# Pooling on VectorE between attention units, seeds written by ScalarE, readout's parts in the recurrence's last chunk

## What is computed

```python
def pool_mixer(u, pool_w, pool_scale):
    cs = jnp.concatenate([jnp.zeros_like(uf[:, :1]), jnp.cumsum(uf, axis=1)], axis=1)
    for gi, w in enumerate(POOL_WINDOWS):
        mean = (jnp.take(csg, hi, axis=1) - jnp.take(csg, lo, axis=1)) / (hi - lo)[None, :, None]
        outs.append((mean - uf[..., sl]).astype(u.dtype) @ pool_w[gi])
    return jnp.concatenate(outs, axis=-1) * pool_scale
```

```python
def step(S, inp):
    S = (S * w_t[:, :, None, :]
         - jnp.einsum('bhij,bhj->bhi', S, kk_t)[..., None] * kka_t[:, :, None, :]
         + v_t[..., None] * k_t[:, :, None, :])
def rwkv_readout(y, r, k_sum, v, g, r_k, ln_g, ln_b, wo, dtype):
    mean = jnp.mean(y, axis=-1, keepdims=True)
    var = jnp.mean(jnp.square(y - mean), axis=-1, keepdims=True)
    yn = ((y - mean) * lax.rsqrt(var + GN_EPS)).reshape(B, L, D_MODEL) * ln_g + ln_b
    bonus = (jnp.sum(r * k_sum * r_k, axis=-1, keepdims=True) * v).reshape(B, L, D_MODEL)
    return ((yn + bonus) * g).astype(dtype) @ wo
```

## Time and profile before

| what | us |
|---|---|
| median of 3 runs | 2590.53 (2588.93 to 2593.68) |
| the profiled run | 2590.95 |
| span of its profile | 2589.1 |
| PE busy in the span | 2378.9 (92%) |
| DVE busy | 1719.1 (66%) |
| ACT busy | 1011.7 (39%) |
| POOL busy | 68.1 (3%) |

### The profile page before, as it was taken

One profiled execution on the slowest core, in us unless ns is written; L12 is line 12 of the kernel. 1 busy time (PEld: TensorE's weight loads), 2 busy tenths in 40 slices (PEclk: granted clock), 3 DMA queues, 4 the chain that ended last, 5 costly groups with the idle time before them and its releaser, 6 DMA issues.

```text
span 2589.1 us, 46659 instructions
## 1 busy us (share of the span) xinstructions
PE 2378.9 (92%) x20102; PEld 1954.2 (75%) x20102; DVE 1719.1 (66%) x3313; ACT 1011.7 (39%) x1879; POOL 68.1 (3%) x70
## 2 busy tenths in 40 slices
PE   6899978999988999999999889898889989998998
PEld 5775457787866578888887789895677889677886
DVE  6966789667646247787773677765365865755576
ACT  2125242313322223543331453344345654644465
POOL 0300000000000000000000000020000011000000
PEclk9899989999998999999998999999989999997999
DMA  7430426555541100000002477640045943003574
GB/s 306 146 114 1 174 103 240 221 221 211 211 154 67 64 1 3 3 4 3 11 4 93 173 272 281 242 164 17 1 186 217 341 182 138 10 1 116 193 295 193
DMA packets 47279, 348.02 MB, mean 134 GB/s; under 512 B 5248, under 2 KB 5248, under 8 KB 5728
## 3 DMA queue, kind: packets, MB, share of 16 engines
q1 hardware_dynamic: 45936, 334.52, 34.6%
q0 software_dynamic: 1136, 10.51, 1.0%
HBM read 343.96 MB, written 1.05 MB: 133 GB/s over the span
## 4 chain that ended last, share of the span: by engine, by line
PE 76%; DVE 16%; ACT 6%; issue 2%; DMA 1%; DVEq 0%; ACTq 0%; POOLq 0%
PE banks L534 23%; PE banks L928 9%; PE banks L1824 6%; DVE arena L613 3%; PE banks L2618 3%; PE banks L2619 3%; PE banks L2620 3%; PE banks L1696 2%; PE banks L1028 2%; PE banks L783 2%; PE banks L1007 2%; PE banks L1897 1%; PE banks L2649 1%; PE banks L2651 1%; PE banks L2650 1%
## 5 line engine op out<-in xcount | busy, mean ns | idle before, releaser
L613 DVE SCALAR_TENSOR_TENSOR arena<-weight_slots,silu_c,arena 128x256 f32<-128x256 f32 x776 | 328.3, 495 | 0.0
L515 DVE TENSOR_TENSOR moe_w_low<-weight_slots,moe_w_high 128x2048 fp32r<-128x2048 f32 x96 | 217.9, 2289 | 70.4 <-ACT moe_w_high L506 69.5
L928 PE MATMUL banks<-arena,weight_slots 128*128 128x256 f32 (+1 forms) x768 | 228.8, 456 | 13.5 <-DVE arena L1577 11.7
L928 PEld LDWEIGHTS banks<-arena,weight_slots 128*128 128x128 f32 x768 | 148.0, 193 | 88.2 <-issue 73.0
L506 ACT ACTIVATE moe_w_high<-weight_slots 128x2048 fp32r<-128x2048 f32 x96 | 181.2, 1911 | 23.7 <-PE banks L2651 19.7
L506 ACT ACTIVATE mlp_w_high<-weight_slots 128x2048 fp32r<-128x2048 f32 x64 | 122.2, 1910 | 171.6 <-PE banks L534 132.3
L515 DVE TENSOR_TENSOR mlp_w_low<-weight_slots,mlp_w_high 128x2048 fp32r<-128x2048 f32 x64 | 146.4, 2287 | 50.7 <-ACT mlp_w_high L506 50.6
L1824 PE MATMUL banks<-weight_slots,arena 64*64 64x64 f32 (+1 forms) x3648 | 147.0, 223 | 18.9 <-ACT arena L1844 13.3
L1824 PEld LDWEIGHTS banks<-weight_slots,arena 64*64 64x64 f32 x3648 | 139.0, 134 | 25.6 <-ACT arena L1844 15.2
L2618 PE MATMUL banks<-moe_w_high,slots_x 128*128 128x512 f32 x320 | 133.3, 416 | 11.8 <-DVE moe_w_low L515 11.8
L2619 PE MATMUL banks<-moe_w_low,slots_x 128*128 128x512 f32 x320 | 129.0, 403 | 0.0
(11 more groups left out here) (389 smaller groups left out, 5193.4 us busy)
## 6 DMA issues: line engine op xcount, KB each, us to landing
weight_slots<-weights SPq DMA_DIRECT2D x318, 1024.0 KB, 4.8
arena<-small POOLq DMA_DIRECT2D x1, 2560.0 KB, 9.0
arena<-x_t POOLq DMA_DIRECT2D x1, 2048.0 KB, 16.5
arena<-bias POOLq DMA_DIRECT2D x1, 2048.0 KB, 9.5
constants<-consts POOLq DMA_DIRECT2D x1, 1410.0 KB, 21.3
out_t<-arena SPq DMA_DIRECT2D x1, 1024.0 KB, 3.9
parameters<-params POOLq DMA_DIRECT2D x1, 775.0 KB, 9.9
arena<-pool_inv POOLq DMA_DIRECT2D x1, 512.0 KB, 10.3
```

Of the source, the lines that this page charges most:

```text
L515: nc.vector.tensor_tensor(self.pair(j)[1], slot(j, 0, SLOT), self.pair(j)[0], ALU.subtract).then_inc(*v.step("used", j))
L613: nc.vector.scalar_tensor_tensor(a_, w, c, a_, ALU.mult, ALU.add).then_inc(*v.step())
L928: ins = nc.tensor.matmul(psum(b, 0, w), slot(j, k, 256, i * P, P), moving(k), start=(k == 0), stop=(k == KT - 1))
```

## The change

Three parts. **Pooling**: the 18 operations leave GpSimd, which only clears the pads, and go to VectorE one by one, behind steps 2 to 13 of LAT (12 of them) and steps 2 to 7 of CON (6). Each waits for the operation before it on VectorE. **Seeds**: for chunks 1 to 7 the seed is no matmul; ScalarE copies it into the PSUM bank at the head of its chunk, `grow` at level 1 waits for that. **Readout**: turned values, bonus and gate move into chunk 7 (two matmuls each at a time, behind the levels and around `u`), with their copies on ScalarE and the small steps on VectorE, where the bias and the gate are folded in; mean removal is one matmul with a matrix `CENTRE`; behind the recurrence stay that matmul, the squares, their sum, root, reciprocal, the spread and 2 steps of 512 columns for each pair of tiles. The square root's table is loaded in chunk 7.

```diff
+        def pool_pads(g):
             g.stage("pooling")
             nc.gpsimd.memset(UP, 0.0).then_inc(*g.step("pads"))
-            g.wait_ge(*after("taken", "ev_in", 3))
...
+        def pool_steps():
+            return [(gi, lv) for gi in range(4) for lv in range(gi + 3)]
+        def pool_vector(v, gi, lv):
+            u = UP[:, gi]
+            src = u if lv == 0 else PT3[:, (lv - 1) % 2]
+            if (gi, lv) == (0, 0):
+                v.wait_ge(*after("taken", "ev_in", 3))
+                v.wait_ge(*after("pool_inv"))
+            v.wait_ge(*v.own)
+            if lv <= gi:
+                up, down = (0, 1) if lv == 0 else (1 << (lv - 1), 1 << (lv - 1))
+                lo, hi = 1 << lv, 288 - (1 << lv)
+                nc.vector.tensor_tensor(PT3[:, lv % 2][:, :, lo:hi], src[:, :, lo + up:hi + up],
+                                        src[:, :, lo - down:hi - down], ALU.add).then_inc(*v.step())
+            elif lv == gi + 1:
                 inv = PINV[:, gi].unsqueeze(1).to_broadcast([P, 2, SEQ])
+                nc.vector.tensor_tensor(PD[:, gi], src[:, :, 16:272], inv, ALU.mult).then_inc(*v.step())
+            else:
+                nc.vector.tensor_tensor(PD[:, gi], PD[:, gi], u[:, :, 16:272], ALU.subtract).then_inc(*v.step("pooled", gi))
...
+        VT, GATE = KK[:, :, SEQ:], KR[:, :, SEQ:]
+        RKS, YL = area(30208, KT, SEQ), area(32256, KT, SEQ)
+        YSQ = area(4096, KT, SEQ)
+        Y_ROOT, Y_SPREAD, CENTRE = area(6144, SEQ)[0:16], area(6400, D)[0:16], area(7424, P)
...
@@ -1882,6 +1894,8 @@
                     pe.wait_ge(*after("taken", *bank_state["holder"][b]))
                 bank_state["holder"][b] = key
                 events.where[key] = b
+                if c:
+                    return
                 pe.wait_ge(*after("inverse_t", c, d, 0))
                 nc.tensor.matmul(psum(b), cn("ident"), flat(XI_OF[c % 2][:, d]), start=True, stop=True).then_inc(
                     *pe.step("seed", c, d))
...
+                if lv == 1 and c:
+                    pe.wait_ge(*after("seeded", c, d))
...
+            def value_turned(part):
+                b = take_bank(pe, ("vt", part), WORK_BANKS)
+                I = cn("ident64")
+                for n in range(2):
+                    p = 2 * part + n
+                    for c in range(4):
+                        for h in range(2):
+                            ins = nc.tensor.matmul(psum(b, n * SEQ + c * 64, 64, half(h)), VP[half(h), 4 + c, p, :],
+                                                   I[half(h), :], start=True, stop=True)
+                ins.then_inc(*pe.step("vt", part))
+            def bonus(part):
+                b = take_bank(pe, ("bonus", part), WORK_BANKS)
+                pe.wait_ge(*after("rks", 2 * part + 1))
+                for n in range(2):
+                    ins = nc.tensor.matmul(psum(b, n * SEQ, SEQ), cn("block_ones"), RKS[:, 2 * part + n], start=True, stop=True)
+                ins.then_inc(*pe.step("bonus", part))
+            def gate(part):
+                b = take_bank(pe, ("gate", part), WORK_BANKS)
+                pe.wait_ge(*after("taken", "low_g"))
+                pe.wait_ge(*after("gate_w2"))
+                for n in range(2):
+                    t = 2 * part + n
+                    ins = nc.tensor.matmul(psum(b, n * SEQ, SEQ), LOW["g2"][:, t * P:(t + 1) * P], GH, start=True, stop=True)
+                ins.then_inc(*pe.step("gate", part))
...
+                    if lv < 5 and c == 7:
+                        value_turned(lv - 1)
+                        bonus(lv - 1)
...
+                if c == 7:
+                    gate(0)
+                    gate(1)
                 for d in range(2):
                     XI, W = XI_OF[c % 2][:, d], WK["U"][:, d]
                     pairs_matmul(pe, ("u", c, d), lambda p, r: [(XI[r, p, :], W[r, p, :])],
                                  ready=[("w_out", c, d), ("inverse_t", c, d, LEVELS - 1)])
+                if c == 7:
+                    gate(2)
+                    gate(3)
...
+            def seeded(c, d):
+                act.wait_ge(*after("inverse_t", c, d, 0))
+                act.wait_ge(*after("inverse_t", c - 1, d, LEVELS - 1))
+                nc.scalar.activation(psum(INVERSE_BANKS[d]), flat(XI_OF[c % 2][:, d]), ACT.Copy).then_inc(
+                    *act.step("seeded", c, d))
+            def gate_out(part):
+                act.wait_ge(*after("gate", part))
+                act.wait_ge(*after("gamma", 7, 1))
+                nc.scalar.activation(GATE[:, 2 * part:2 * part + 2], psum(bank_of(("gate", part))).rearrange(
+                    "p (a b) -> p a b", b=SEQ), ACT.Copy).then_inc(*act.step("taken", "gate", part))
...
@@ -2002,6 +2072,9 @@
                 return
             for c in range(8):
                 ahead = c < 7
+                if c:
+                    for d in range(2):
+                        seeded(c, d)
...
+                    if lv == 1 and not ahead:
+                        load_table(act, ACT.Sqrt)
+                    if lv < 5 and not ahead:
+                        part = lv - 1
+                        act.wait_ge(*after("vt", part))
+                        act.wait_ge(*after("beta", 7, 1))
+                        nc.scalar.activation(VT[:, 2 * part:2 * part + 2], psum(bank_of(("vt", part))).rearrange(
+                            "p (a b) -> p a b", b=SEQ), ACT.Copy).then_inc(*act.step("taken", "vt", part))
...
+                if not ahead:
+                    for part in range(2):
+                        gate_out(part)
...
+            def value_bonus(part):
+                v.wait_ge(*after("bonus", part))
+                v.wait_ge(*after("taken", "vt", part))
+                two = VT[:, 2 * part:2 * part + 2]
+                tt(two, psum(bank_of(("bonus", part))).rearrange("p (a b) -> p a b", b=SEQ), two, mul).then_inc(
+                    *v.step("taken", "bonus", part))
...
+                        for t in (2 * lv - 2, 2 * lv - 1):
+                            stt(RKS[:, t], RR[:, t], pr("rk", t, 1), WK["KS"][:, t], mul, mul).then_inc(*v.step("rks", t))
...
+                if not ahead:
+                    spread_vector(v, Y_SPREAD)
+                    stt(CENTRE, cn("block_ones"), -1.0 / HD, cn("ident"), mul, add).then_inc(*v.step("centre"))
+                    for t in range(KT):
+                        v.wait_ge(*after("taken", "gate", t // 2))
+                        stt(VT[:, t], VT[:, t], pr("lnb", t, 1), GATE[:, t], add, mul).then_inc(*v.step())
...
@@ -2210,90 +2316,58 @@
             v.mark("recurrence_done")
-        VT = area(16896, KT, SEQ)
...
         def readout_tensor(pe):
             pe.stage("readout")
-            I = cn("ident64")
+            pe.wait_ge(*after("recurrence_done"))
             for part in range(4):
-                b = take_bank(pe, ("vt", part))
-                pe.wait_ge(*after("recurrence_done"))
+                b = take_bank(pe, ("yc", part), range(6))
                 for n in range(2):
-                    p = 2 * part + n
...
+                    ins = nc.tensor.matmul(psum(b, n * SEQ, SEQ), CENTRE, WK["Y"][:, 2 * part + n], start=True, stop=True)
+                ins.then_inc(*pe.step("yc", part))
             b = take_bank(pe, ("y_var",), [6])
             for t in range(KT):
-                pe.wait_ge(*after("yc_square", t))
-                ins = nc.tensor.matmul(psum(b, 0, SEQ, slice(0, 16)), head_rows(t), Q1[:, t], start=(t == 0),
+                pe.wait_ge(*after("yc_square", t // 2))
+                ins = nc.tensor.matmul(psum(b, 0, SEQ, slice(0, 16)), head_rows(t), YSQ[:, t], start=(t == 0),
                                        stop=(t == KT - 1))
             ins.then_inc(*pe.step("y_var"))
-            for t in range(KT):
...
+            for part in range(4):
+                b = take_bank(pe, ("y_spread", part), range(6))
                 pe.wait_ge(*after("y_inverse"))
-                nc.tensor.matmul(psum(b, 0, SEQ), head_columns(t), RD[0:16, 0], start=True, stop=True).then_inc(
...
+                for n in range(2):
+                    ins = nc.tensor.matmul(psum(b, n * SEQ, SEQ), head_columns(2 * part + n, Y_SPREAD), Y_ROOT,
+                                           start=True, stop=True)
+                ins.then_inc(*pe.step("y_spread", part))
         def readout_scalar(act):
             act.stage("readout")
             for part in range(4):
-                act.wait_ge(*after("vt", part))
...
+                act.wait_ge(*after("yc", part))
+                nc.scalar.activation(YSQ[:, 2 * part:2 * part + 2], psum(bank_of(("yc", part))).rearrange(
+                    "p (a b) -> p a b", b=SEQ), ACT.Square).then_inc(*act.step("yc_square", part))
             act.wait_ge(*after("y_var"))
-            nc.scalar.activation(RD[0:16, 0], psum(bank_of(("y_var",)), 0, SEQ, slice(0, 16)), ACT.Sqrt,
```

(29 more changed lines are left out.)

81 lines of the change are left out of this document (12 added, 69 removed).

## The result

The changed kernel takes 2563.67 us (median of 4 runs, 2562.20 to 2565.26); the kernel before, timed beside it, 2592.11 (4 runs, 2588.93 to 2596.86). The ratio is 0.9895, with a 95% interval of 0.988 to 0.991: 28.4 us between the medians. 2560 had been forecast, with a range of 2551 to 2575. The profiled execution has a span of 2560.1 us against 2589.1, so 29.0 us are to be explained, where the sum in the prediction had 30.6.

The account below looks back on a forecast made before the run. PE, busy 92% of the span, was taken as the bound, gains coming where it waits or works needlessly. 11.8 - 3.0 + 12.5 + 9.3 = 30.6 us off 2590.95 gave 2560.4, median 2560, range 2551 to 2575.

Parts of the forecast that it names:

- Pooling off GpSimd: Projection: VectorE no longer slowed by GpSimd, so PE's block begins at 114.5 instead of 124.55 us; gain 11.8 us.
- Pooling on VectorE: Attentions: ten LAT units grow by 0.3 us each, CON's hide the operations; cost 3.0 us.
- Seeds: Recurrence: `grow` starts at the seeds' place, 1.92 us in chunks 1 to 6, 1.0 in chunk 7; gain 12.5 us.
- Readout: Last chunk and readout: 35.6 us before becomes 26.3 after, with 1.6 for a clock fall; gain 9.3 us.
- 1: Projection: VectorE's slow stretch isn't GpSimd's doing (weights' DMA writes too), the wait stays; 2572 us, chance 0.08.
- 2: Recurrence: seeds bring nothing, because masks or ScalarE's copies end level 1, not `grow`; 2572.5 us, chance 0.08.
- 3: Readout: its parts only move; banks, waits in chunk 7 and a long clock fall eat the rest; 2569 us, chance 0.10.
- 4: LAT and CON: VectorE operations in units make PE wait and keep the clock at half; slower, 2622 us, chance 0.04.
- (a): Projection: L613's chain at 97 us takes 5.6 us, PE has no wait near 113 to 124, attention begins 11.8 us earlier.
- (b): Attentions: LAT's unit is 2.95 us between steps 4 and 13, VectorE free of waits; CON's stays 2.44.
- (c): Recurrence: `grow` follows `z` directly in chunks 1 to 7; the chunks' heads lie 1.9 us closer.
- (d): Chunk 7 is 11.3 us longer but for the seed; its end to `wo` 15 us instead of 34; clock before `wo`.

Follow-up runs that it names:

- GpSimd late: Kernel before, pooling still on GpSimd but begun only after VectorE split the projection's last weights, before LAT: 2581.29 us against 2591.99, ratio 0.9955.
- the dose: Kernel before with the last six of GpSimd's 18 pooling operations left out: 2590.62 us against 2596.18, ratio 0.9989.
- the pooling alone: Kernel before with the pooling on VectorE between the attentions' units, nothing else changed: 2586.94 us against 2591.99, ratio 0.9977.
- the second profile of the same kernel: Changed kernel run once more, unaltered, on the same chip as later kernels: 2563.15 us.

## Why the prediction was right, and where it wasn't

*Pooling off GpSimd*: forecast 11.8 us, measured 11.96. The block was to begin at 114.5 and began at 114.37. Shown by GpSimd late and by the dose.

*Pooling on VectorE*: forecast 3.0 us, measured 2.2 in the profile (11.96 - 9.73), with CON free as forecast: its units stay at 2.44 us, and of VectorE's 0.91 us of idle time 0.15 to 0.19 are left. An operation was 0.69 to 0.76 us (0.72 had been taken). It cost less because nine distances between scores grew, not ten, and by less: from 2.68 to 2.92 us on average, 0.24 and not 0.3. The first two scores behind the half clock still followed each other at PE's pace (2.80 and 2.66 us). The upper bound was of the wrong kind, though: I had bounded this term by VectorE's time (8.6), and what made it 9.4 with the pooling alone is the clock: some 7 us of the 9.4.

*Seeds*: forecast 12.5 us, measured 20.57 - 7.84 = 12.7, and 12.7 alone. Right, with the 0.1 us of slack at the second direction sufficient: PE shows no wait in chunks 1 to 6. Chunk 7 gave 0.9 us where 1.0 had been taken.

*Readout*: forecast 9.3 us, measured 6.2 (26.79 - 20.57). The mechanism was right and two terms of its sum were too small. Chunk 7 and its end grew by 12.6 us, not 11.25: from the first `grow` to the centred values it is 42.46 us (1320.76 to 1363.22), before 29.90 (1341.33 to 1371.23). Two matmuls of the bonus take 1.06 us between other work and not the 0.91 that the dense row L2234 gives, which makes 0.6 us in four places; four gate matmuls take 1.92 and not 1.83, 0.2 in two places. The level with the first `grow` has 0.3 us more, and 0.2 are spread. Behind the recurrence 9.6 us were forecast and are 9.60. From the spreads to the end of `wo`'s three groups it is 17.6 us (1372.82 to 1390.43), where 15.85 were forecast: the fall of the clock costs 3.4 us, not 1.6, and in the second profile of the same kernel 4.9 (7.19 and 11.96 us for the two rows, less the 14.25 at full clock). I had placed it near zero because LAT recovered quickly; LAT's recovery was itself the short end of 6.8 to 23.9 us. I also read the stretch before as 12.5 us, which was the window that I had asked for: it lasted 17.1 us and reached into `wo`.

*What the sum left out*: 1.9 us are lost between the attentions and the recurrence and 2.2 are won behind `wo`, in stages that the change doesn't touch. The falls of the clock lie elsewhere in the two traces. In the first stage both have the same 65 us at half clock, but the changed kernel has a fall at 707 to 714 us that the one before has not, and the one before has as much more at 773 to 797 us. Behind `wo`, falls at 1490, 1575 and 1770 us stand only in the trace before. In the second profile of the changed kernel the fall at 707 us is there again, and some 2 us are lost there again. The three late ones are there too (1465, 1551 and 1745 us), and only 0.1 us is won behind `wo`: those 2.2 us belong to the one execution and not to the change. That 3 to 4 us of this were possible stood in the range, not in the sum. That the two cancelled to 0.3 is luck.

*The rivals.* 1 falls, by two experiments and by the 6 us of slow instructions without weights. 2 falls: 12.7 us alone. 3 falls: 7.4 us alone. 4, the slower side, had hold of something real: LAT did stay at half clock for 23.9 us in the run with the pooling alone, at 4.9 us a unit, and that cost about 7 us more than a stretch of 6.8 us does. But it did not reach CON, it was not the operations between the units that kept the clock down, and 7 us are far from the 30 from which it would decide.

*What would show it.* (a) came as written. So did (b), with 2.92 us instead of 2.95 and two units at PE's pace, and (c) in chunks 1 to 6; in chunk 7 `grow` did not follow `z` directly, as the prediction's own sum has it. Of (d), chunk 7 was longer than said (12.6), and from its end to `wo` it is 13.9 us (15 had been said); the clock fell at 1375.8 us, ahead of `wo`, and most of its price was paid in `wo`. PE showed no wait on VectorE's bonus steps.

The median is 3.7 us above the forecast. The sum explains 1.6 of it (30.6 forecast, 29.0 found): the readout's 3.1 too much, less 1.5 that the other terms and the stages outside gave. Another 1.5 us is that the profiled run (2562.20) lies below the median of its four runs, 0.4 that the forecast had put the median below the profiled run, and 0.2 lie outside the span.
